# RWKV chunk stage: 16x16 diagonal blocks on VectorE, the rest in four rounds of 64x64 products on TensorE

## What is computed

```
def step(state, inp):
    r_t, w_t, k_t, v_t, kk_t, a_t = inp
    sa = jnp.einsum('bhvk,bhk->bhv', state, -kk_t)
    state = (state * w_t[:, :, None, :]
             + sa[..., None] * (kk_t * a_t)[:, :, None, :]
             + v_t[..., None] * k_t[:, :, None, :])
    return state, jnp.einsum('bhvk,bhk->bhv', state, r_t)
```

## Time and profile before

| | us |
|---|---|
| median of three runs | 3257.96 |
| lowest, highest | 3241.26, 3276.20 |
| the profiled execution, its own time | 3223.39 |
| its span, first to last instruction | 3221.6 |
| PE, DVE, ACT busy | 2839.6 (88%), 1463.9 (45%), 782.4 (24%) |
| first product of the four chunk stages at | 1399.23, 1600.74, 1801.98, 2000.23 |
| first product of the scans behind them at | 1504.59, 1705.89, 1907.36, 2104.72 |

### The profile page before, as it was taken

One profiled execution on the slowest core, in us unless ns is written; L12 is line 12 of the kernel. 1 busy time (PEld: TensorE's weight loads), 2 busy tenths in 40 slices (PEclk: granted clock), 3 DMA queues, 4 the chain that ended last, 5 costly groups with the idle time before them and its releaser, 6 DMA issues. The chain is left out here.

```text
span 3221.6 us, 47743 instructions
## 1 busy us (share of the span) xinstructions
PE 2839.6 (88%) x19150; PEld 2613.4 (81%) x19150; DVE 1463.9 (45%) x2807; ACT 782.4 (24%) x1527; POOL 118.0 (4%) x165
## 2 busy tenths in 40 slices
PE   4489999999996999768788787887789999999995
PEld 2289999999996999457575575757789999999995
DVE  1453333333337663184674746723453333333335
ACT  1231111111113211243334433322231111111112
POOL 0000000000000000000303003010000000000000
PEclk8799999999997999767869778688899999999997
DMA  8511111111100222211010110105111111111101
GB/s 344 221 53 40 39 39 39 39 50 41 39 20 27 83 92 91 111 24 33 13 28 26 31 32 17 25 2 177 33 53 40 39 39 39 39 52 39 39 20 59
DMA packets 190799, 182.70 MB, mean 57 GB/s; under 512 B 43955, under 2 KB 163550, under 8 KB 190686
## 3 DMA queue, kind: packets, MB, share of 16 engines
q1 hardware_dynamic: 190416, 180.97, 17.4%
q10 hardware_dynamic: 270, 0.09, 0.0%
HBM read 153.05 MB, written 27.98 MB: 56 GB/s over the span
## 5 line engine op out<-in xcount | busy, mean ns | idle before, releaser
L126 PE MATMUL ff_ps<-h_hi,ff_wlo 128*128 128x384 f32 x2112 | 710.4, 336 | 7.5 <-ACT ff_s L602 7.5
L127 PE MATMUL ff_ps<-h_lo,ff_whi 128*128 128x384 f32 x2112 | 709.3, 336 | 0.0
L128 PE MATMUL ff_ps<-h_hi,ff_whi 128*128 128x384 f32 x2112 | 708.7, 336 | 0.0
L650 DVE TENSOR_TENSOR ff_s<-ff_ps,ff_s 128x384 f32<-128x384 f32 x132 | 73.6, 557 | 752.5 <-PE ff_ps L128 751.2
L126 PEld LDWEIGHTS ff_ps<-h_hi,ff_wlo 128*128 128x128 f32 x2112 | 399.7, 189 | 8.1 <-ACT ff_s L602 8.1
L127 PEld LDWEIGHTS ff_ps<-h_lo,ff_whi 128*128 128x128 f32 x2112 | 399.5, 189 | 0.0
L128 PEld LDWEIGHTS ff_ps<-h_hi,ff_whi 128*128 128x128 f32 x2112 | 399.4, 189 | 0.0
L127 PE MATMUL ff_ps<-ff_ulo,ff_whi 128*128 128x384 f32 x1056 | 352.7, 334 | 0.0
L126 PE MATMUL ff_ps<-ff_uhi,ff_wlo 128*128 128x384 f32 x1056 | 352.7, 334 | 0.0
L128 PE MATMUL ff_ps<-ff_uhi,ff_whi 128*128 128x384 f32 x1056 | 352.7, 334 | 0.0
L602 ACT ACTIVATE ff_s<-ff_ps 128x384 f32<-128x384 f32 x132 | 65.0, 492 | 740.9 <-PE ff_ps L128 740.9
(11 more groups left out here) (271 smaller groups left out, 3672.3 us busy)
## 6 DMA issues: line engine op xcount, KB each, us to landing
md_w<-w_mod SPq DMA_DIRECT2D x9, 4096.0 KB, 24.4
ff_raw<-ffn_w_gate SPq DMA_DIRECT2D x44, 512.0 KB, 4.6
ff_raw<-ffn_w_up SPq DMA_DIRECT2D x44, 512.0 KB, 3.9
ff_raw<-ffn_w_down SPq DMA_DIRECT2D x44, 512.0 KB, 3.6
pj_raw<-w_in SPq DMA_DIRECT2D x19, 512.0 KB, 4.1
z_dram<-pj_zo SPq DMA_DIRECT2D x15, 576.0 KB, 2.9
rw_rkv<-z_dram SPq DMA_DIRECT2D x12, 576.0 KB, 5.4
x_dram<-x SPq DMA_DIRECT2D x1, 4608.0 KB, 21.8
```

The source lines that it names most:

```text
L126: pe.matmul(out, w_lo, x_hi, start=start, stop=False)
L127: pe.matmul(out, w_hi, x_lo, start=False, stop=False)
L128: return pe.matmul(out, w_hi, x_hi, start=False, stop=stop)
L650: dve.tensor_tensor(hid[:, t % 2, :], ps[:, 2 + t % 2, 0:CW], silu[:, t % 2, :], ALU.mult)\
```

## The change

- Two 64-element masks are added to the constants (C_OFF): one outside the 16x16 diagonal blocks for each direction. `rw_first` zeroes four DRAM arrays for the inverses and their transposes: a GpSimd memset of 128x1152 and four flat writes of 576 KB.
- A new job n comes first: N itself, in pairs of 64x64 products (one for each head, in opposite quarters of the array). ACT copies it raw to SBUF; SP writes it flat to DRAM at once, ahead of any mask, and fetches the diagonal blocks with 8 DMAs a direction (288 runs of 64 bytes each). DVE keeps N without its diagonal blocks (`outside`).
- `invert` works on 72 lanes with two 16x16 blocks each, 15 rounds. Direction 1 has its own order of rounds and needs no transposes. A copy (`turn`) makes the transposed inverse.
- SP writes both to DRAM with 8 DMAs each (288 runs of 64 bytes) and loads them back as full 64x64 matrices, flat, 576 KB each.
- PE then joins the four blocks: f = N_off times D, w = f times D (DVE subtracts it from D), q = f times w's result, x = f times q (DVE adds it). All are pairs of 64x64 products. u's products now stand in pairs too, a becomes a product with the identity, and the idle products ahead of f are gone.
- The order of the jobs is new: n0 n1 g0 v s, g1 among b0 a0 z0, then f0 b1 w0 a1 q0 z1, then f1 x0 w1 u0 q1 y0 x1 u1 y1.

```diff
+            @block.gpsimd
+            def _(pool):
+                pool.memset(rw.work[:, 0:T], 0.0).then_inc(zeros, 1)
...
+def diagonal(dram, h):
+    step = BI * T + BI
+    v = dram[h * HS * T:h * HS * T + HS // BI * step].rearrange("(b q) -> b q", q=step)[:, 0:BI * T]
+    return v.rearrange("b (i c n) -> b i c n", i=BI, n=HS)[:, :, :, 0:BI]
...
+    many = lambda k, d, n: [(k, d, q) for q in range(n)]
+    jobs = many("n", 0, NB) + many("n", 1, NB) + many("g", 0, G1) + many("v", 0, NG) + [("s", 0, 0)]
+    between = many("b", 0, NG) + many("a", 0, NB) + many("z", 0, NB)
+    for n in range(NG):
+        jobs += [("g", 1, 2 * n), ("g", 1, 2 * n + 1)] + between[2 * n:2 * n + 2]
+    jobs += many("f", 0, NB) + many("b", 1, NG) + many("w", 0, NB) + many("a", 1, NB) + many("q", 0, NB) + many("z", 1, NB)
+    jobs += [job for k, d, n in (("f", 1, NB), ("x", 0, NB), ("w", 1, NB), ("u", 0, G1 // 2), ("q", 1, NB), ("y", 0, NB),
+                                 ("x", 1, NB), ("u", 1, G1 // 2), ("y", 1, NB)) for job in many(k, d, n)]
     name = lambda k, d, n: f"{k}{d}_{n}"
-    on_dve = lambda k, d, n: k == "g" or (k in "fwuy" and d == 1 and n % 2 == 1)
...
+    on_act = lambda k, d, n: k in "nvsbazfqy" or k == "u" and n % 2 == 0
+    on_dve = lambda k, d, n: k in "ngwx" or k == "u" and n % 2 == 1
...
-                def out_of(d, src):
-                    for b in range(2):
-                        sp.dma_start(nd[d, :, b].rearrange("u r t -> r u t"), src(slice(B * b, B * b + B))).then_inc(n_out[d], 16)
-                    sp.wait_ge(n_out[d], 32)
-                    sp.dma_start(ni[d].rearrange("p i j -> p (i j)"), nd[d].rearrange("u b r t -> (u b) (r t)"))\
-                      .then_inc(n_in[d], 16)
-                def back(d, dst):
-                    dve_t.wait(sp, f"minus{d}_{B - 2}")
-                    sp.dma_start(wd[d].rearrange("u b r t -> (u b) (r t)"), wi[d].rearrange("p i j -> p (i j)"))\
-                      .then_inc(w_out[d], 16)
-                    sp.wait_ge(w_out[d], 16)
-                    for b in range(2):
-                        sp.dma_start(dst(slice(B * b, B * b + B)), wd[d, :, b].rearrange("u r t -> r u t")).then_inc(w_in[d], 16)
-                dve_t.wait(sp, name("g", 0, 2 * NG - 1))
-                out_of(0, lambda rows: gu[rows, 0, :, rows])
-                dve_t.wait(sp, "nt1")
-                out_of(1, lambda rows: nt[rows])
-                pool_t.wait(sp, "w0")
-                back(0, lambda rows: wu[rows, 0, :, rows])
-                back(1, lambda rows: nat[1][rows])
+                flat = lambda t, d: t[d][0:P * T].rearrange("(p t) -> p t", t=T)
+                lanes = lambda t, h, b: t[(2 * h + b // 2) * NCH:(2 * h + b // 2 + 1) * NCH, b % 2]
+                blocks = lambda t, h, b: diagonal(t, h)[b].rearrange("i c j -> c i j")
+                HB = [(h, b) for h in range(2) for b in range(HS // BI)]
                 for d in range(2):
-                    sp.wait_ge(w_in[d], 32)
+                    act_t.wait(sp, name("n", d, NB - 1))
+                    sp.dma_start(flat(nd, d), work[:, d * T:(d + 1) * T]).then_inc(n_out[d], 16)
+                for d in range(2):
+                    sp.wait_ge(n_out[d], 16)
+                    for h, b in HB:
+                        sp.dma_start(lanes(ni[d], h, b), blocks(nd[d], h, b)).then_inc(n_in[d], 16)
+                for d in range(2):
+                    dve_t.wait(sp, f"minus{d}_{BI - 2}")
+                    for h, b in HB:
+                        sp.dma_start(blocks(ud[d], h, b), lanes(wi[d], h, b)).then_inc(u_out[d], 16)
+                    dve_t.wait(sp, f"t{d}")
+                    for h, b in HB:
+                        sp.dma_start(blocks(utd[d], h, b), lanes(wit[d], h, b)).then_inc(t_out[d], 16)
+                    sp.wait_ge(t_out[d], 16 * len(HB))
+                    sp.dma_start(xt[d].rearrange("p c n -> p (c n)"), flat(utd, d)).then_inc(t_in[d], 16)
+                    sp.wait_ge(u_out[d], 16 * len(HB))
+                    sp.dma_start(x[d].rearrange("p c n -> p (c n)"), flat(ud, d)).then_inc(u_in[d], 16)
+                for d in range(2):
+                    sp.wait_ge(t_in[d], 16)
+                    sp.wait_ge(u_in[d], 16)
...
+                def heads(out, q, w, v):
+                    for j in range(NU):
+                        for h in range(2):
+                            last = pe.matmul(out[rows_of[h], j * HS:(j + 1) * HS], w(rows_of[h], h, q * NU + j),
+                                             v(rows_of[h], h, q * NU + j), start=True, stop=True)
+                    return last
...
                     elif k == "f":
                         if q == 0:
-                            keep_clock(pe, sb, out, 512, 4)
-                            dve_t.wait(pe, f"nat{d}_1")
...
+                            copied(pe, "n", d, NB - 1)
+                            pe.wait_ge(t_in[d], 16)
+                        last = heads(out, q, lambda rows, h, c: noff[d][rows, c, :], lambda rows, h, c: xt[d][rows, c, :])
+                    elif k in "wq":
+                        copied(pe, *{"w": ("f", d, q), "q": ("w", d, q)}[k])
+                        if k == "w" and q == 0:
+                            pe.wait_ge(u_in[d], 16)
+                        last = heads(out, q, lambda rows, h, c: f[d][rows, c, :], lambda rows, h, c: x[d][rows, c, :])
+                    elif k == "x":
+                        copied(pe, "q", d, q)
+                        last = heads(out, q, lambda rows, h, c: f[d][rows, c, :], lambda rows, h, c: r1[d][rows, c, :])
                     else:
+                        copied(pe, "x", d, q)
+                        copied(pe, "a", d, q)
+                        last = heads(out, q, lambda rows, h, c: at[rows, d, c, :], lambda rows, h, c: x[d][rows, c, :])
...
+                def outside(d, q):
+                    act_t.wait(dve, name("n", d, q))
+                    mask = sb["cst"][:, C_OFF + d * HS:C_OFF + (d + 1) * HS].unsqueeze(1).to_broadcast([P, NU, HS])
+                    dve_t.did(name("n", d, q), dve.tensor_tensor(
+                        noff[d][:, q * NU:(q + 1) * NU, :],
+                        ps[:, bank["n", d, q], 0:NU * HS].rearrange("p (c n) -> p c n", c=NU), mask, ALU.mult))
...
                 def invert(d, a, b):
                     for r in range(a, b):
-                        j = B - 1 - r
-                        sh = [2 * U, j, B - j]
                         if r == 0:
-                            dve.wait_ge(n_in[d], 16)
+                            dve.wait_ge(n_in[d], 16 * 8)
                             pool_t.wait(dve, "one")
-                        if r:
+                            if d:
+                                dve_t.wait(dve, f"minus0_{BI - 2}")
+                        else:
                             dve_t.wait(dve, f"minus{d}_{r - 1}")
-                        elif d:
-                            dve_t.wait(dve, f"minus0_{B - 2}")
-                        t = tmp[:, 0:j, j:B]
-                        dve_t.did(f"times{d}_{r}", dve.tensor_tensor(t, ni[d][:, 0:j, j:j + 1].to_broadcast(sh),
-                                                                     wi[d][:, j:j + 1, j:B].to_broadcast(sh), ALU.mult))
+                        j = r if d else BI - 1 - r
+                        rows, cols = (slice(j + 1, BI), slice(0, j + 1)) if d else (slice(0, j), slice(j, BI))
+                        shape = [LANES, 2, rows.stop - rows.start, cols.stop - cols.start]
+                        t = tmp[:, :, rows, cols]
+                        dve_t.did(f"times{d}_{r}", dve.tensor_tensor(t, ni[d][:, :, rows, j:j + 1].to_broadcast(shape),
+                                                                     wi[d][:, :, j:j + 1, cols].to_broadcast(shape), ALU.mult))
                         dve_t.wait(dve, f"times{d}_{r}")
-                        dve_t.did(f"minus{d}_{r}", dve.tensor_tensor(wi[d][:, 0:j, j:B], wi[d][:, 0:j, j:B], t, ALU.subtract))
+                        dve_t.did(f"minus{d}_{r}", dve.tensor_tensor(wi[d][:, :, rows, cols], wi[d][:, :, rows, cols], t,
+                                                                     ALU.subtract))
+                def turn(d):
+                    dve_t.wait(dve, f"minus{d}_{BI - 2}")
+                    dve_t.did(f"t{d}", dve.tensor_copy(wit[d], wi[d].rearrange("p k i j -> p k j i")))
+                def product(k, d, q):
+                    pe_t.wait(dve, name(k, d, q))
+                    xs = x[d][:, q * NU:(q + 1) * NU, :]
+                    dve_t.did(name(k, d, q), dve.tensor_tensor(
+                        xs, xs, ps[:, bank[k, d, q], 0:NU * HS].rearrange("p (c n) -> p c n", c=NU),
+                        ALU.subtract if k == "w" else ALU.add))
+                for d in range(2):
+                    for n in range(NB):
+                        outside(d, n)
                 for n in range(G1):
                     masked(0, n)
```

(62 more changed lines are left out.)

172 lines of the change are left out of this document (75 added, 97 removed).

## The result

| | before | after |
|---|---|---|
| median, us | 3265.86 (4 runs, 3241.26 to 3276.20) | 3154.05 (4 runs, 3145.03 to 3159.90) |
| span of the profiled execution | 3221.6 | 3152.5 |
| the four chunk stages | 98.1, 97.8, 98.1, 96.6: 390.6 | 79.3, 76.9, 77.1, 73.2: 306.5 |
| scan and turn between them | 103.4, 103.4, 100.1: 307.0 | 101.2, 121.4, 99.6: 322.2 |
| ahead of the first stage, behind the last | 1399.2, 1124.8 | 1399.3, 1124.5 |

The two medians stand as 0.966 to 1; the recorded ratio is 0.9736, 95% interval 0.9696 to 0.9776, because it leaves out slow executions, those over 1.5% above the fastest of the same kernel, which here are runs of the kernel before. Two differences have to be told apart: 111.8 us between the medians and 69.1 between the profiled executions. The stages give 84.1, the stretches between them take 15.2 back.

What follows compares the result with a forecast made beforehand. In the chunk stage, run four times, DVE's inversions and masks set most of the path. Each stage falls from 98.1 to 81.0 us, plus 2.4 at the scan: 78 off the 3258.0 median gives 3180, range 3135 to 3270.

Steps and rivals of the forecast that it cites:

- (a): Chunk stage's opening: n, raw N through DRAM, masks; inversion 0 starts at 16.2 us, 1.4 later than before.
- (b): Inversion 0 on DVE: 30 steps, 8.8 us, with direction 1's 12 masks between, 6.7; ends at 31.7.
- (c): Inverse's way back through DRAM: 16 stores landed after 9.5 us, flat load 4.1; 13.6 in all, f0 at 45.3.
- (d): PE jobs f0 to z1: half clock for f0, b1's transposes raise it, then full; 16.0 us, to 61.3.
- (e): PE jobs f1 to y1: nine phases at full clock, 18.9 us; last copy 0.8, stage ends at 81.0.
- (f): Scan's eight opening products after the stage: 3.7 us at full clock instead of 6.1, saving 2.4.
- rival (1): Clock stays at half from f0 to the stage's end: stage 103.8 us, kernel 3281, the same within 1%; chance 0.14.
- (2): Rival: 24 small DRAM transfers a stage are slow; at 1.33 us each the gain is gone, worst 3370; chance 0.09.
- (3): Rival: small DRAM transfers a little slow, 0.75 us each instead of 0.48; gain 14 a stage, 3202; chance 0.12.
- (4): Rival: paired products raise the clock already within f0 or n; 18 us more gained, 3162; chance 0.12.

Runs made afterwards that it cites:

- e7: e1's order with direction 0's inverse stores on ACT's queue and the transposes stored first on SP's; 3121.25 us, ratio 0.9553.
- e1: Kernel after with jobs b1, a1, z1 moved ahead of f0 and the later jobs reordered; 3118.02 us, ratio 0.9551.
- e5: Kernel after plus 96 unused 64x64 products ahead of f0, in pairs: one row half (stages 1 to 3), opposite quarters (stage 4); run once, time not read.
- e6: Kernel after plus 96 unused products ahead of f0: pairs on both row halves, one column half (stages 1 to 3), single quarter (stage 4); time not read.
- e8: Kernel before with the idle product in each scan step 384 columns wide instead of 256; 3234.85 us, ratio 0.9968.
- e9: Kernel after with the idle product in each scan step 384 columns wide instead of 256; 3148.43 us.
- e3: Kernel after with eight more small stores a direction, ahead of the wait for the transposed inverse; 3174.23 us, ratio 0.9717.

## Why the prediction was right, and where it was off

Faster was right, 3154 lies in the range, and it is 26 us below the forecast. Its steps, in us a stage (measured: mean of four, from the same marks):

| step | predicted | measured |
|---|---|---|
| (a) start to inversion 0 | 16.2 | 14.2 (12.95, 15.4, 15.3, 13.3) |
| (b) inversion 0 | 15.5 | 13.9 |
| (c) way back to f0 | 13.6 | 12.1 |
| (d), (e) f0 to the end | 35.7 | 36.4 (40.2, 35.7, 35.8, 33.9) |
| stage | 81.0 | 76.6 |
| (f) saved at the scan's opening | 2.4 | 1.4 (2.2, 0.6, 0.5, 2.3) |

- **(a) and (b), the mis-sized term is the mask.** 0.556 was read from a row in which DVE kept PE's pace at half clock for its first half; DVE's own price is 0.47. That is 1.0 us in (a) and 1.0 of 1.6 in (b). The 30 steps took 8.5 us in inversion 1, where no masks stand between them (8.8 predicted), so the four-dimensional views cost no more an element. Another 0.6 in (a) is the start of the masks, taken as 9.2 and found at 7.4, 9.7, 9.7 and 7.7. It follows the clock, which n raises while it runs, at + 4.3, + 8.1, + 7.7 and + 5.1; in stages 2 and 3 PE also stood idle 0.8 and 1.1 us in n with nothing shown to release it.
- **(c)** 16 issues at 0.44 instead of 0.48, the last landing 1.3 us behind them, load 4.0 (predicted 4.1). The sum holds for one queue. That the issue itself is what costs, as I reasoned, didn't hold: issued faster from two queues, the same stores landed no sooner (e7).
- **(d)** was right in its sum (f0 to f1 15.4 in the mean, 16.0 predicted) and wrong in its reason. Half clock over f0 and full from about b1 on came true, but b1 isn't needed for it (e1); pairs like f0's are enough (e5, e6). So the Trainium skill's rule on transposes (TensorE: Matmul & The Clock Gate, Part 4: PE-mode transpose) was no danger to this stage, right or not: rival (1) needed the paired products to be too little, and they weren't. Against the rule stands the row from which I argued: in the kernel before PE ran nothing but transposes for 12.4 us ahead of the rise at 1431.8. What share b1 had in the rise of the kernel after, no run takes apart. Full-clock phases start 2.1 us apart, 0.70 a group, as predicted. In stage 1 alone PE stood 1.72 us in z1 with nothing shown to release it, and the clock fell for 6.8 us; that is the 40.2.
- **(e)** f1 to the last copy took 22.1, 20.8, 21.2 and 19.8 us, 19.7 predicted. f1's slack was predicted as 5.5 and was 5.7, 3.1, 0.8 and 1.3: the match of stage 1 is luck, since PE lost 1.7 us there before f1. The load of direction 1 was never waited for, but in stages 3 and 4 it was close, and e1 met it.
- **(f)** is half of what I took. PE stands idle 2.0 us at the turn to the scan, and in stages 2 and 3 the clock fell in the opening products (5.37 instead of 3.67). Of the 2.3 us behind stage 4 only 0.3 is left at the kernel's end.
- **The sum and the median.** Predicted 17.1 + 2.4 = 19.5 a stage, found 21.0 + 1.4 = 22.4: 90 us in place of 78, of which the profiled execution gave back some 19 in scan 2 and 2 behind the last opening. I subtracted the 78 from the median of before as if its distance from the profiled execution (35 us) were fixed. It is not: the runs of before lie near 3223, 3241, 3259 and 3275, in steps of 16 to 18 us, and a scan at half clock costs 12 to 18. Of the 111.8 us between the medians 86 are the change (e8 and e9; 2.6% by the recorded ratio is as much), and some 25 are left. They fit scans that lose the clock more often in the kernel before. From the 3258 that I started from, the drop is 104: 8 of the 26 by which the forecast was too high are the change itself, 86 instead of 78, and some 18 the scans. That 3180 came as near as that is part luck. That each step of the ladder is one scan is inferred: the one profiled execution of before lies on the lowest step and lost none.
- **Rivals.** (1) fell; (2) and (3) fell with SP's rows and e3 (0.44 and 0.42 us a store); (4) is the mechanism that the runs show, in n and in f0, but not at its price of 4.5 us a stage: the early rise gave about 0.6 in (a), and in f0 it came only 3.3 to 6.1 us after the beginning, at the end of f0 or in b1, worth some 1.2 (f0 and b1 together 7.1, 6.3, 6.1 and 5.9 instead of 7.6).

## What to carry to other kernels

Before a duration is taken from a row, ask whose pace it is: a row of twelve masks behind PE at half clock is PE's price. A small scattered store cost 0.44 us here as issued from one queue, so count the stores between the last result and the first load; a second queue doesn't make them land sooner. Look at direction 1's chain before shortening direction 0's. And when runs of one kernel lie on a ladder, find the rung of the profiled one before subtracting from a median.

## What the runs showed of the hardware

- With PE busy without a gap in each case, TensorE's clock rose from 1.2 to 2.4 GHz 3.1 to 5.4 us after the beginning of 64x64 products in pairs on both row halves; it didn't in 10.5 us of pairs on one row half, nor in 20.7 us of products in a single quarter (e5, e6). Begun at full clock, singles kept it: z did in the kernel before, for 4.2 and 4.4 us at a stretch.
- Two products in different quarters run side by side, on the same rows too: 96 products took 20.71 us in one quarter and 10.51 in two on one row half, at the same clock (e6, e5).
- Sixteen stores of 288 pieces of 64 bytes had landed 8.0 to 8.5 us after the first was issued, from one queue (after) and from two (e7). Eight issues on one queue took 3.4 us, in stage 1 4.69 and 5.29 while flat loads were under way.
